# Expert weights of a routed mixture: loaded over one hardware DMA queue, or over two

## The chip, the cores and the metric

The kernel runs on one core of a Trainium2 chip. The metric is the device time of one execution, in microseconds. Before the change it is 2785.39 us, the median of three runs (2783.75 to 2786.51). A program on a single core has no other core to wait for.

## The reference, cut to what matters

The reference is a trunk of two layers. Each layer has a token mixer and then a mixture of 16 experts over 512 latent tokens and, in the first layer, also 256 context tokens. Everything is float32. The change is in the experts alone:

```
def ec_moe(h, w_router, w_gate, w_up, w_down):
    B, T, D = h.shape                            # D = 1024
    cap = EC_FACTOR * T // N_EXPERTS             # 64 latent tokens, 32 context tokens an expert
    aff = softmax(einsum('btd,de->bte', h, w_router))
    gate, idx = lax.top_k(swapaxes(aff, 1, 2), cap)
    xe = h[idx]
    hid = silu(einsum('becd,edf->becf', xe, w_gate)) * einsum('becd,edf->becf', xe, w_up)
    ye = einsum('becf,efd->becd', hid, w_down) * gate[..., None]
    return zeros(T, D).at[idx].add(ye)
```

Each expert has three matrices of 1024 x 1024 float32 (w_gate, w_up, w_down), 4 MB each, 12 MB in all. A layer reads 16 times 12 MB, and each expert's weights serve only 64 or 96 tokens.

## The kernel before, in words

The program is written engine by engine; an engine runs its own list in order and meets the others through semaphores alone. Nothing reorders the lists. The mixer, norms and routing take the stretches from 0 to about 970 us and from about 1510 to 2270 us of the span. The two expert phases lie at about 970 to 1510 us (layer 0, latent and context tokens) and 2270 to 2765 us (layer 1, latent tokens alone).

In an expert phase SBUF holds six slots of 2 MB. A slot s holds one half (512 rows) of one matrix of one expert, called a unit here and written (expert, slot): slots 0 and 1 hold the first and second half of w_gate, 2 and 3 those of w_up, 4 and 5 those of w_down. Slots 0 to 2 lie in the buffer `ring_lo`, slots 3 to 5 in `zone`, and rows of a profile name a unit by matrix and buffer. In layer 1 (`near_rows`) a unit is read as 16 KB pieces, in layer 0 as 4 KB pieces.

TensorE runs a hardware loop over the 16 experts (from `with pe.Fori(0, NE)`, helpers `in_half` and `out_half`, matmul lines L836 for gate and up, L846 for down). It takes the slots in the order 0 to 5. Before each it waits for `w_ready(s)`, which the transfer of the unit raises by 16; after each slot, or in layer 0 after each pair of slots, it raises `unit_done`. Between up and down stand the transposes of the hidden rows (L886) and those of the next expert's gathered tokens (L826). In layer 1 there are also eight small matmuls (`place`, L855) that put the previous expert's output rows in their places.

ScalarE's loop has few steps for each expert: the silu of the gate result (L1197, in layer 0 also L1201 for context tokens), the copy of the transposed hidden rows (L1203, raises `hidL`), and the scaled copy of the expert's output (L1208, in layer 0 also L1210, raises `ytm`). GpSimd issues the token gather (L1787) and, in layer 0, the scatter with addition (L1805); both are indirect DMAs on a queue of their own.

All weight transfers are issued by SyncE. Expert 0's six units are issued before the phase. Then comes the loop of L1923: for expert e and slot s it waits until `unit_done` says that expert e-1 has used slot s (L1925), then until the unit issued two before this one has landed (L1929; the semaphore of slot s-2), and issues the unit (L1912 in layer 0, L1910 in layer 1). So in this loop at most two units are under way at a time, both on SyncE's hardware queue (q1 in the profile). ScalarE has a hardware queue too (q10), which the mixer uses for 22 small transfers.

Of the kernel before, what the change touches and what calls it, by code (L numbers as in the profile page):

```python
# [14 lines left out]
P = 128  # L15
# [11 lines left out]
NE, FF = 16, 1024  # L27
# [47 lines left out]
def build(nc, A, out):  # L75
    ctx = ExitStack()
    with ctx:
# [5 lines left out]
        def sem(name):  # L83
            if name not in made:
                made[name] = ctx.enter_context(nc.semaphore(name))
            return made[name]
# [28 lines left out]
        def slot_ap(s):  # L115
            return ring_lo[:, s * SLOT:(s + 1) * SLOT] if s < 3 else zone[:, (s - 3) * SLOT:(s - 2) * SLOT]
# [70 lines left out]
        o = Z0  # L187
# [17 lines left out]
        o = Z0  # L205
# [14 lines left out]
        o = Z0  # L220
# [44 lines left out]
        def bank(j):  # L265
            return PS[j // 2][:, (j % 2) * 512:(j % 2) * 512 + 512]
# [21 lines left out]
        for l in range(DEPTH):  # L288
            n = [0]
# [14 lines left out]
            for q in range(12):  # L304
                c = C_BG + 256 * q
# [22 lines left out]
        def w_ready(s):  # L328
            return sem(f"w_ready{s}")
# [4 lines left out]
        def phase_end(eng, n):  # L334
            eng.drain().then_inc(sem("phase"), 1)  # L335
            eng.wait_ge(sem("phase"), 4 * n)
        NPH = 12

        def nt(l):
            return NT if l == 0 else LT  # L340
# [4 lines left out]
        def streams(l):  # L345
            return [(0, 0, S)] + ([(1, S, CTX)] if l == 0 else [])
# [9 lines left out]
        def near_rows(l):  # L356
            return l > 0
# [27 lines left out]
            return st  # L385

        POOL_ORDER = (3, 2, 1, 0)

        block = ctx.enter_context(nc.Block())

# [2 lines left out]
        def _(pe):  # L393
            mm, tr = nc.tensor.matmul, nc.tensor.transpose

            def unit(key):
                src, slot, count, _, _ = units[key]
                pe.wait_ge(w_ready(slot), 16 * count)
                return slot_ap(slot)
# [42 lines left out]
            for l in range(DEPTH):  # L442
# [31 lines left out]
                for n, (src, k) in enumerate([(src, k) for src in (hi_r, lo_r) for k in range(KD)]):  # L474
                    q = k % 4
                    for _, t0, tw in both():
                        i = mm(PS[3][32 * q:32 * q + 32, t0:t0 + tw], gw[:, k, :], src[:, k, t0:t0 + tw].bitcast(F32),
                               start=(n < 4), stop=(n >= 12), skip_group_check=True)
# [150 lines left out]
                def features(name, tag, g0, sts, free, order=range(KB)):  # L629
                    for half in range(2):  # L630
                        w = split_unit(l, name, half)
                        for f in order:
                            if half == 0 and free:
                                pe.wait_ge(sem(free), l * PER[free] + g0 + f - 3)
                            for _, t0, tw in sts:
                                for k in range(4):
                                    i = cols3(PS[f], 4 * half + k, k, f, t0, tw, w, half == 0 and k == 0, half == 1 and k == 3)
                            if half:
                                i.then_inc(sem(tag), 1)
                            elif f == order[-1]:  # L640
                                i.then_inc(sem("half"), 1)
                        released[l, name, half] = (tag, l * PER[tag] + g0 + KB) if half else \
                            ("half", l * PER["half"] + SPLITS.index((name, 0)) // 2 + 1)
# [86 lines left out]

                features("pu", "pup", 0, streams(l), None, POOL_ORDER)
                pe.wait_ge(sem("pw_in"), l * PER["pw_in"] + 16)
                for n, gi in enumerate(POOL_ORDER):
                    pe.wait_ge(sem("pin"), l * PER["pin"] + n + 1)
# [182 lines left out]
        def _(act):  # L917
# [17 lines left out]
            for l in range(DEPTH):  # L935
# [64 lines left out]
                for j in range(NT):  # L1000
                    c = FW[j]
# [19 lines left out]
                for n in range(12):  # L1021
                    r, c = n % 2, (FW, BWD)[n % 2][n // 2]
# [104 lines left out]

                for n, f in enumerate(POOL_ORDER):
                    act.wait_ge(sem("pup"), l * PER["pup"] + n + 1)
# [3 lines left out]
                    act.drain().then_inc(sem("pu"), 1)  # L1133
                for n, gi in enumerate(POOL_ORDER):
                    act.wait_ge(sem("pmap"), l * PER["pmap"] + n + 1)
# [52 lines left out]

                ns = nslot[l]
                act.drain().then_inc(sem("ytm"), 1)  # L1190
                with act.Fori(0, NE) as e:
                    if first:
                        act.wait_ge(sem("gate_L"), e + 1)
                    else:
                        act.wait_ge(sem("unit_done"), l * PER["unit_done"] + 6 * e + 2)
                    act.wait_ge(sem("hid"), l * PER["hid"] + e + 1)
                    A_(gsil[:, 0:512], bank(2), ACT.Silu).then_inc(sem("gsil"), 1)  # L1197
                    if first:
                        act.wait_ge(sem("unit_done"), 6 * e + 2)
                        act.wait_ge(sem("hid_c"), e + 1)  # L1200
                        A_(gsil[:, 512:768], bank(4)[:, 0:256], ACT.Silu).then_inc(sem("gsil_c"), 1)  # L1201
                    act.wait_ge(sem("hid_T"), l * PER["hid_T"] + e + 1)
                    A_(hidL.rearrange("p b g m -> p (b g m)"), bank(6), ACT.Copy).then_inc(sem("hidL"), 1)  # L1203
                    act.wait_ge(sem("iprev"), l * PER["iprev"] + e + 1)
                    if first:
                        act.wait_ge(sem("ig_free"), e + 1)
                    act.wait_ge(sem("unit_done"), l * PER["unit_done"] + 6 * e + 6)
                    i = A_(ytm[:, 0:512], bank(3), ACT.Copy, scale=gcur[:, 0:1])  # L1208
                    if first:
                        i = A_(ytm[:, 512:768], bank(5)[:, 0:256], ACT.Copy, scale=gcur[:, 1:2])  # L1210
                    i.then_inc(sem("ytm"), 1)
                phase_end(act, ph + 12)
                for t in range(nt(l) + 1):
                    if t < nt(l):
# [16 lines left out]
        def _(dve):  # L1231
# [34 lines left out]
            for l in range(DEPTH):  # L1266
# [229 lines left out]
                dve.drain()  # L1496
                for n, gi in enumerate(POOL_ORDER):
                    w = WINDOWS[gi]
# [316 lines left out]
        def _(sp):  # L1815
# [20 lines left out]
            for l in range(DEPTH):  # L1836
# [61 lines left out]
                for s, t0, t1 in [(0, 0, LT), (1, LT, NT)][:len(streams(l))]:  # L1898
                    src = (A["x"][0], A["ctx"][0])[s] if l == 0 else x_dram[l]
                    sp.dma_start(x_sb[:, t0:t1, :], src.rearrange("(t p) d -> p t d", p=P)).then_inc(sem("x_back"), 16)  # L1900


                exp_src = [(A["w_gate"], 0), (A["w_gate"], 512), (A["w_up"], 0), (A["w_up"], 512),
                           (A["w_down"], 0), (A["w_down"], 512)]

                def expert_unit(e, s):
                    w, c = exp_src[s]
                    src = w[l][bass.ds(e, 1), c:c + 512, :]
                    if near_rows(l):
                        sp.dma_start(slot_ap(s), src.rearrange("o (p k) n -> p (o k n)", p=P)).then_inc(w_ready(s), 16)  # L1910
                    else:
                        sp.dma_start(slot_ap(s).rearrange("p (k n) -> p k n", k=4),  # L1912
                                     src.rearrange("o (k p) n -> p (o k) n", p=P)).then_inc(w_ready(s), 16)
                for s in range(6):
                    if s < 3:
                        sp.wait_ge(sem(last[s][0]), last[s][1])
                    elif s == 3:
                        sp.wait_ge(sem("phase"), 4 * (NPH * l + 9))
                    expert_unit(0, s)
                if near_rows(l):  # L1920
                    sp.wait_ge(sem("phase"), 4 * (NPH * l + 11))
                    sp.dma_start(iota, A["iota"]).then_inc(sem("iota_in"), 16)
                with sp.Fori(1, NE) as e:  # L1923
                    for s in range(6):
                        sp.wait_ge(sem("unit_done"), l * PER["unit_done"] + 6 * e + (s - 5))  # L1925
                        sp.sem_inc(sem("sp_turn"), 1)

                        s2, back = (s - 2) % 6, 1 if s < 2 else 0
                        sp.wait_ge(w_ready(s2), 16 * e + 16 * (moe_base[l][s2] + 1 - back))  # L1929
                        sp.sem_inc(sem("sp_turn"), 1)  # L1930
                        expert_unit(e, s)

                for s in range(6):
                    last[s] = ("unit_done", l * PER["unit_done"] + 6 * NE - 5 + s)
# [41 lines left out]
```

## Time and profile before

| | |
|---|---|
| median of the runs | 2785.39 us |
| profiled execution, its own time | 2786.34 us |
| span of its trace | 2784.6 us |
| mean granted TensorE clock | 0.942 |
| TensorE busy | 2431.1 us, 87% of the span |
| ScalarE busy | 616.1 us, 22% |
| bytes on SyncE's queue q1 | 561.18 MB |
| bytes on ScalarE's queue q10 | 5.31 MB |
| read from HBM | 574.53 MB |

The span runs from the first to the last instruction of the profiled execution; 1.7 us of its own time lie outside. A transfer's "us to landing" runs from its issue to the moment when its semaphore has the full count. Engine names: PE is TensorE's matmuls, PEld its weight loads, DVE VectorE, ACT ScalarE, POOL GpSimd, SPq and ACTq the instruction queues of SyncE and ScalarE. Where a row of TensorE has a bracket, the number in it is the idle time just before the row, with what ended it. PEclk is the share of full clock that TensorE was granted.

### The profile page before, as it was taken

The page shows a single profiled execution, that of the slowest core. Times are in us where ns is not written, and L with a number is a line of the kernel's source. Part 1 is how long each engine was busy: PE and PEld are TensorE (multiplying, and loading weights), DVE is VectorE, ACT ScalarE, POOL GpSimd, SP SyncE. Part 2 cuts the span into 40 slices and gives each one's busy share as a digit, 9 for nine tenths or more (in the row PEclk, how much of TensorE's full clock was granted, in tenths as well). Part 3 has the DMA queues.
Part 4 walks back from the last instruction along what each step waited for, and adds up shares of the span by engine and source line. Part 5 has one row for each costly group of instructions (what it writes and reads, how often), then busy time and mean ns, then how long its engine had stood idle before and what let it go on. Part 6 is the DMA issues. An engine that isn't in the chain of part 4 may idle for free.

```text
span 2784.6 us, 38818 instructions
## 1 busy us (share of the span) xinstructions
PE 2431.1 (87%) x16038; PEld 1540.2 (55%) x16038; DVE 729.7 (26%) x1401; ACT 616.1 (22%) x1038; POOL 551.8 (20%) x304
## 2 busy tenths in 40 slices
PE   3987979899999399999997597997899859988886
PEld 2766867788874244444443475776688433333332
DVE  3245035301001511111111426135210142322224
ACT  3233234322111211111111423233321121101011
POOL 1232231324420011111111223231455000000000
PEclk7999999999999699999998798999999979999998
DMA  6261331122140599999999245332223369999996
GB/s 225 88 232 61 121 99 35 46 68 68 48 156 0 207 347 387 389 391 391 390 390 362 89 150 194 82 99 72 68 91 99 109 268 403 410 411 403 408 409 263
DMA packets 177524, 593.92 MB, mean 213 GB/s; under 512 B 13928, under 2 KB 55280, under 8 KB 165040
## 3 DMA queue, kind: packets, MB, share of 16 engines
q1 hardware_dynamic: 164080, 561.18, 53.9%
q0 software_dynamic: 10304, 25.99, 3.4%
q10 hardware_dynamic: 3040, 5.31, 0.6%
q8 instruction: 76, 1.25, 0.2%
q14 instruction: 24, 0.20, 0.0%
HBM read 574.53 MB, written 21.05 MB: 214 GB/s over the span
## 4 chain that ended last, share of the span: by engine, by line
PE 47%; DMA 36%; issue 6%; DVE 5%; ACT 3%; SPq 1%; POOLq 1%; POOL 1%; DVEq 0%; ACTq 0%
PE ps L418 15%; DMA ring_lo<-in_w_gate 12%; DMA zone<-in_w_up 11%; DMA zone<-in_w_down 10%; PE ps L413 9%; PE ps L760 6%; PE ps L778 5%; PE ps L836 2%; PE ps L427 2%; PE ps L693 1%; DMA ring_lo<-in_ada_w 1%; PE ps L710 1%; POOLq L335 1%; PE ps L598 1%; DVE zone L1413 1%
## 5 line engine op out<-in xcount | busy, mean ns | idle before, releaser
L418 PE MATMUL ps<-hi_r,ring_r 128*128 128x512 f32 (+1 forms) x1792 | 477.0, 355 | 18.2 <-POOLq L335 14.8
L836 PE MATMUL ps<-ring_lo,zone 128*32 128x256 f32 (+1 forms) x3072 | 440.4, 494 | 31.1 <-DMA ring_lo<-in_w_gate 26.9
L418 PEld LDWEIGHTS ps<-hi_r,ring_r 128*128 128x128 f32 x1792 | 318.6, 191 | 67.1 <-POOLq L335 16.1
L1682 POOL TENSOR_TENSOR ring_r<-ring_lo,ring_r 128x2048 fp32r<-128x2048 f32 x52 | 239.6, 4610 | 482.2 <-ACT ring_r L929 481.8
L836 PEld LDWEIGHTS ps<-ring_lo,zone 128*32 128x32 f32 (+1 forms) x3072 | 156.9, 124 | 307.9 <-issue 280.3
L418 PE MATMUL ps<-lo_r,ring_r 128*128 128x512 f32 (+1 forms) x896 | 316.7, 353 | 0.0
L846 PE MATMUL ps<-zone 128*64 128x512 f32 (+1 forms) x2048 | 290.9, 495 | 0.9
L413 PE MATMUL ps<-ring_r,hi_r 128*128 128x512 f32 x736 | 234.5, 400 | 21.8 <-DVEq L335 21.8
L1787 POOL DMA_INDIRECT zone<-xn_dram,zone x36 | 40.5, 1124 | 860.0 <-DVE zone L1654 773.4
L846 PEld LDWEIGHTS ps<-zone 128*64 128x64 f32 (+1 forms) x2048 | 110.9, 125 | 164.0 <-issue 143.7
L418 PEld LDWEIGHTS ps<-lo_r,ring_r 128*128 128x128 f32 x896 | 170.7, 190 | 23.5
L413 PEld LDWEIGHTS ps<-ring_r,hi_r 128*128 128x128 f32 x736 | 138.3, 192 | 51.1 <-DVEq L335 22.1
L1528 DVE TENSOR_TENSOR zone<-zone,ps 128x768 f32<-128x768 f32 (+1 forms) x48 | 39.4, 821 | 427.3 <-ACT zone L1159 427.3
L836 PE MATMUL ps<-zone 128*32 128x256 f32 (+1 forms) x1024 | 146.9, 487 | 2.7 <-DMA zone<-in_w_up 2.7
L413 PE MATMUL ps<-ring_r,lo_r 128*128 128x512 f32 x368 | 145.5, 395 | 0.0
L778 PE MATMUL ps<-ring_lo,zone 128*128 128x512 f32 x320 | 137.7, 592 | 0.0
L1614 DVE TENSOR_TENSOR zone<-zone,ps 128x512 f32<-128x512 f32 x136 | 84.3, 681 | 198.9 <-PE ps L855 198.8
L760 PE MATMUL ps<-br_lo,ring_r 128*128 128x512 f32 (+1 forms) x480 | 126.4, 355 | 0.0
L929 ACT ACTIVATE ring_r<-ring_lo 128x2048 fp32r<-128x2048 f32 x48 | 91.6, 1914 | 132.4 <-DMA ring_lo<-in_w_in 111.7
L760 PE MATMUL ps<-br_up,ring_r 128*128 128x512 f32 (+1 forms) x384 | 104.2, 358 | 3.8 <-DVE br_lo L1520 3.8
L778 PEld LDWEIGHTS ps<-ring_lo,zone 128*128 128x128 f32 x320 | 60.6, 190 | 75.8 <-issue 75.8
L836 PEld LDWEIGHTS ps<-zone 128*32 128x32 f32 (+1 forms) x1024 | 52.5, 123 | 90.2 <-issue 79.2
(272 smaller groups left out, 2584.7 us busy)
## 6 DMA issues: line engine op xcount, KB each, us to landing
ring_lo<-in_w_gate SPq DMA_DIRECT2D x64, 2048.0 KB, 10.9
zone<-in_w_down SPq DMA_DIRECT2D x64, 2048.0 KB, 10.1
ring_lo<-in_w_up SPq DMA_DIRECT2D x32, 2048.0 KB, 11.7
zone<-in_w_up SPq DMA_DIRECT2D x32, 2048.0 KB, 11.6
ring_lo<-in_w_in SPq DMA_DIRECT2D x52, 1024.0 KB, 5.3
ring_lo<-in_ada_w SPq DMA_DIRECT2D x24, 2048.0 KB, 11.7
ring_lo<-in_w_branch SPq DMA_DIRECT2D x24, 512.0 KB, 6.3
zone<-v_dram SPq DMA_DIRECT2D x128, 64.0 KB, 2.0
```

Of the source, the lines that this page charges most:

```text
L413: i = mm(dst, a[:, k, t * P:(t + 1) * P], b[:, kk, :], start=start and n == 0, stop=stop and n == 2)
L418: i = mm(dst[:, t0:t0 + tw], b[:, kk, f * P:(f + 1) * P], a[:, k, t0:t0 + tw], start=start and n == 0, stop=stop and n == 2)
L427: i = mm(bank(b)[32 * q:32 * q + 32, (j % 4) * P:(j % 4 + 1) * P], csil[:, k, :], w[:, k, q * P:(q + 1) * P], start=(k == 0), stop=(k == K ...
L760: i = mm(pb[:, t0:t0 + tw], w[:, k, (f % 2) * P:(f % 2 + 1) * P], b[:, k, t0:t0 + tw], start=(k == 0 and x == 0), stop=(k == KB - 1 and x ...
L778: i = mm(PS[2 + t % 2][:, j * 512:(j + 1) * 512], acc[:, k, t * P:(t + 1) * P], w[:, k, :], start=(k == 0), stop=(k == KD - 1))
L836: i = mm(bank(((2, 4), (3, 5))[s // 2][gi])[j * M:(j + 1) * M, 0:W], xeT[:, k, c0:c0 + M], w[:, k % 4, j * W:(j + 1) * W], start=(k == 0), ...
L846: i = mm(bank((3, 5)[gi])[j * M:(j + 1) * M, 0:W], hidL[:, k % 4, k // 4, :] if gi == 0 else hidC[:, k % 2, k // 2, :], w[:, k % 4, j * W: ...
L929: A_(unit_hi(slot, ring_r), unit_lo(slot), ACT.Copy).then_inc(sem("w_hi"), 1)
L1528: V.tensor_tensor(dst[:, 0:TW(l)], sg[f % 2][:, 0:TW(l)], PS[(f % 2) * 2][:, 0:TW(l)], ALU.mult).then_inc(sem("mg_free"), 1)
L1614: i = V.tensor_tensor(xn[:, t, 512 * j:512 * j + 512], xn[:, t, 512 * j:512 * j + 512], bank(HOT_BANKS[t % 2][j]), ALU.add)
L1682: G.tensor_tensor(unit_lo(slot, ring_r), unit_lo(slot), unit_hi(slot, ring_r).bitcast(F32), ALU.subtract)\
L1787: G.indirect_dma_start(xe[0:ns, :], None, xn_dram[l][0:TW(l), :], bass.IndirectOffsetOnAxis(ap=icur[0:ns, 0:1], axis=0)).then_inc(sem("xe_ ...
```

## The change: which engine issues which unit

The helper `expert_unit` moves out of SyncE's block, so that two engines can call it. SyncE's loop now issues only slots 0, 2 and 4; its two waits are written as before, so the unit of slot s-2 is now the one that SyncE itself issued last. ScalarE issues slots 1, 3 and 5 of the next expert at three points of its loop: slot 1 behind the silu, slot 3 behind the copy that raises `hidL` and a wait for `unit_done`, slot 5 behind the copy that raises `ytm`. These three have no wait for a landing. Expert 0 is still issued by SyncE, and ScalarE's last expert stands outside the loop, without transfers.

```
+        def expert_unit(eng, l, e, s):
+            w, c = exp_src[s]
+            src = w[l][bass.ds(e, 1), c:c + 512, :]
...
-                with act.Fori(0, NE) as e:
+
+                def expert(e, more):
...
+                    if more:
+                        expert_unit(act, l, e + 1, 1)
                     act.wait_ge(sem("hid_T"), l * PER["hid_T"] + e + 1)
                     A_(hidL.rearrange("p b g m -> p (b g m)"), bank(6), ACT.Copy).then_inc(sem("hidL"), 1)
+                    if more:
+                        act.wait_ge(sem("unit_done"), l * PER["unit_done"] + 6 * e + 4)
+                        expert_unit(act, l, e + 1, 3)
...
                     i.then_inc(sem("ytm"), 1)
+                    if more:
+                        expert_unit(act, l, e + 1, 5)
+                with act.Fori(0, NE - 1) as e:
+                    expert(e, True)
+                expert(NE - 1, False)
...
                 with sp.Fori(1, NE) as e:
-                    for s in range(6):
+                    for s in (0, 2, 4):
                         sp.wait_ge(sem("unit_done"), l * PER["unit_done"] + 6 * e + (s - 5))
                         sp.sem_inc(sem("sp_turn"), 1)
 
                         s2, back = (s - 2) % 6, 1 if s < 2 else 0
                         sp.wait_ge(w_ready(s2), 16 * e + 16 * (moe_base[l][s2] + 1 - back))
                         sp.sem_inc(sem("sp_turn"), 1)
-                        expert_unit(e, s)
+                        expert_unit(sp, l, e, s)
```

On SyncE the loop of layer 1 stood in this order before (`w_ready0` is the landing of slot 0, and so on):

```order
L1929 ISA [waits unit_done]
L1910 ISA [waits w_ready4]
L1910 DMA ring_lo<-in_w_gate 128x4096
L1925 REGISTER_ALU
L1910 ISA [waits unit_done,w_ready5]
L1910 DMA ring_lo<-in_w_gate 128x4096
L1925 REGISTER_ALU
L1929 REGISTER_ALU [waits unit_done]
L1910 DMA ring_lo<-in_w_up 128x4096 [waits w_ready0]
```

The same place of SyncE after the change:

```order
L1941 ISA [waits unit_done]
L396 ISA [waits w_ready4]
L396 DMA ring_lo<-in_w_gate 128x4096
L1937 REGISTER_ALU
L1941 REGISTER_ALU [waits unit_done]
L396 DMA ring_lo<-in_w_up 128x4096 [waits w_ready0]
L1937 REGISTER_ALU
L1941 REGISTER_ALU [waits unit_done]
L396 DMA zone<-in_w_down 128x4096 [waits w_ready2]
```

Between the transfers into slots 0 and 2 stood the one into slot 1; it is gone, while slot 2 still waits for slot 0's landing, slot 4 for slot 2's and slot 0 for slot 4's.

ScalarE's loop of layer 1 before:

```order
L1197 ACTIVATE zone<-ps 128x512 [waits hid]
L1202 REGISTER_ALU
L1203 ACTIVATE zone<-ps 128x512 [waits hid_T]
L1207 REGISTER_ALU [waits iprev]
L1208 ACTIVATE zone<-ps,zone 128x512 [waits unit_done]
```

ScalarE's loop of layer 1 after the change:

```order
L1210 ACTIVATE zone<-ps 128x512 [waits hid]
L396 ISA
L396 DMA ring_lo<-in_w_gate 128x4096
...
L1218 ACTIVATE zone<-ps 128x512 [waits hid_T]
L1220 REGISTER_ALU
L396 DMA zone<-in_w_up 128x4096 [waits unit_done]
L1225 REGISTER_ALU [waits iprev]
L1226 ACTIVATE zone<-ps,zone 128x512 [waits unit_done]
L396 DMA zone<-in_w_down 128x4096
```

A transfer now stands behind each of the three compute steps, and each waits in ScalarE's list for what stands ahead of it.

## Rows read from the trace of the kernel before

**Rows 1.** The page: 40 slices of 69.6 us, and the chain by engine.
```profile
GB/s 225 88 232 61 121 99 35 46 68 68 48 156 0 207 347 387 389 391 391 390 390 362 89 150 194 82 99 72 68 91 99 109 268 403 410 411 403 408 409 263
PE 47%; DMA 36%; issue 6%; DVE 5%; ACT 3%; SPq 1%; POOLq 1%; POOL 1%; DVEq 0%; ACTq 0%
```
**Rows 2.** Timeline, SyncE's issues in layer 1: start us, duration, queue, line, transfer, count.
```profile
2279.71 3.70 SPq L1910 DMA_DIRECT2D ring_lo<-in_w_gate  x2
...
2515.42 0.33 SPq L1910 DMA_DIRECT2D zone<-in_w_up  x1
2520.31 5.23 SPq L1910 DMA_DIRECT2D zone<-in_w_down  x2
...
2719.45 5.21 SPq L1910 DMA_DIRECT2D ring_lo<-in_w_gate  x2
```
**Rows 3.** Timeline, SyncE's issues in layer 0.
```profile
978.87 2.02 SPq L1912 DMA_DIRECT2D ring_lo<-in_w_gate  x2
...
1236.36 0.37 SPq L1912 DMA_DIRECT2D zone<-in_w_up  x1
1241.48 7.21 SPq L1912 DMA_DIRECT2D zone<-in_w_down  x2
...
1459.23 5.47 SPq L1912 DMA_DIRECT2D ring_lo<-in_w_gate  x2
```
**Rows 4.** Timeline, TensorE: hidden-row transposes once an expert, and waits for weights.
```profile
1224.63 0.66 PE L886 MATMUL ps<-cst,zone 128*128 128x128 f32 x4
1258.05 0.66 PE L886 MATMUL ps<-cst,zone 128*128 128x128 f32 x4
...
1454.02 3.65 PE L836 MATMUL ps<-zone 128*64 128x512 f32 x16 [0.56 <-DMA zone<-in_w_up]
...
2350.40 0.72 PE L886 MATMUL ps<-cst,zone 128*128 128x128 f32 x4 [1.06 <-DVE zone L1645]
2378.17 0.72 PE L886 MATMUL ps<-cst,zone 128*128 128x128 f32 x4 [1.06 <-DVE zone L1645]
...
2547.05 5.35 PE L836 MATMUL ps<-ring_lo,zone 128*64 128x512 f32 x16 [2.10 <-DMA ring_lo<-in_w_gate]
```
**Rows 5.** Line view of L1910 (layer 1): issue to landing.
```profile
DMA to landing us min/median/max: 7.8/9.7/31.3
```
**Rows 6.** Line view of L1912 (layer 0): issue to landing.
```profile
DMA to landing us min/median/max: 7.9/11.7/32.3
```
**Rows 7.** Windows: busy us (count) by engine, then PEclk, DMA share, GB/s.
```profile
2506.00:2511.00 5.00, 3.81 (x18) 1.15 (x16) 0.15 (x1) 0.69 (x1) 0.00 (x0) 1.00 1.01 308
2512.00:2529.00 17.00, 14.96 (x68) 4.85 (x66) 5.51 (x10) 1.88 (x2) 0.00 (x0) 1.00 1.01 428
1220.00:1230.00 10.00, 9.95 (x102) 5.03 (x100) 3.54 (x8) 0.60 (x1) 0.95 (x1) 1.00 1.03 410
1677.00:1680.00 3.00, 2.06 (x20) 1.80 (x22) 1.63 (x5) 1.73 (x7) 2.28 (x2) 1.00 1.04 398
1680.00:1682.00 2.00, 1.26 (x18) 0.93 (x16) 1.93 (x5) 1.53 (x6) 0.00 (x0) 1.00 1.06 396
```
**Rows 8.** Timeline, ScalarE's queue in the mixer of layer 1: one load issued.
```profile
1676.45 0.33 ACTq L979 DMA_DIRECT2D zone<-u_dram  x1
```
**Rows 9.** DMA issues by line: KB each, median us to landing.
```profile
zone<-u_dram ACTq DMA_DIRECT2D x20, 256.0 KB, 6.5
zone<-in_iota SPq DMA_DIRECT2D x1, 256.0 KB, 2.6
```
**Rows 10.** Timeline, ScalarE in one expert of layer 1.
```profile
2520.46 0.60 ACT L1197 ACTIVATE zone<-ps 128x512 f32<-128x512 f32 x1
2531.89 0.60 ACT L1203 ACTIVATE zone<-ps 128x512 f32<-128x512 f32 x1 [10.83 <-PE ps L886]
2540.02 0.69 ACT L1208 ACTIVATE zone<-ps,zone 128x512 f32<-128x512 f32 x1 [7.53 <-PE ps L846]
```
**Rows 11.** Line view of L1912: duration of the issuing instruction, ns min/median/max.
```profile
L1912 SPq DMA_DIRECT2D zone<-in_w_down x32: 372/373/4780, 906.9 to 1488.4; - x32
```

More of the change, by code:

```diff
@@ L387, in build @@
         POOL_ORDER = (3, 2, 1, 0)
+        exp_src = [(A["w_gate"], 0), (A["w_gate"], 512), (A["w_up"], 0), (A["w_up"], 512),
+                   (A["w_down"], 0), (A["w_down"], 512)]
+        def expert_unit(eng, l, e, s):
+            w, c = exp_src[s]
+            src = w[l][bass.ds(e, 1), c:c + 512, :]
+            if near_rows(l):
+                eng.dma_start(slot_ap(s), src.rearrange("o (p k) n -> p (o k n)", p=P)).then_inc(w_ready(s), 16)
+            else:
+                eng.dma_start(slot_ap(s).rearrange("p (k n) -> p k n", k=4),
+                              src.rearrange("o (k p) n -> p (o k) n", p=P)).then_inc(w_ready(s), 16)
         block = ctx.enter_context(nc.Block())
@@ L1900, in _ @@
                     sp.dma_start(x_sb[:, t0:t1, :], src.rearrange("(t p) d -> p t d", p=P)).then_inc(sem("x_back"), 16)
[L1903 to L1913, printed above, removed]
                 for s in range(6):
@@ L1918, in _ @@
                         sp.wait_ge(sem("phase"), 4 * (NPH * l + 9))
-                    expert_unit(0, s)
+                    expert_unit(sp, l, 0, s)
                 if near_rows(l):
```

## The prediction

> **What bounds the kernel now.** I read the page's slices first. GB/s shows two plateaus, 387 to 391 and 403 to 411, which are the two expert phases, and the chain puts 36% of the span on DMA [rows 1]. The change is in these phases alone, so the question is whether their pace is set by TensorE, by the transfers, or by the waits between them.
>
> The pace of the transfers comes from SyncE's issues. In layer 1 the first unit of an expert is issued at 2279.71 for expert 1 and at 2719.45 for expert 15 [rows 2]: 439.7 us over 14 experts, 31.4 us each. In layer 0 it is 978.87 and 1459.23 [rows 3]: 480.4 over 14, 34.3 us each. The pace of TensorE comes from its transposes, once an expert. Where it waits for no weights it takes 33.4 us an expert in layer 0 (1224.63 to 1258.05) and 27.8 in layer 1 (2350.40 to 2378.17) [rows 4]. So transfers set the pace in both phases, by 0.9 us an expert in layer 0 and by 3.6 in layer 1. TensorE lives on the units loaded ahead at first, then waits: 0.56 us for a half of w_up late in layer 0, 2.10 for the second half of w_gate in layer 1 [rows 4].
>
> Are the DMA engines full, then, or only late? Full: in layer 1 they stand at a share of 1.01 and 428 GB/s for 17 us on end, in layer 0 at 1.03 and 410 [rows 7]. Two units under way at a time suffice for that: the next issues follow 4.89 us apart (2515.42 to 2520.31) [rows 2], 5.12 in layer 0 [rows 3]. Six such units are 29.3 of the 31.4 us, and 30.7 of the 34.3. The other 2.1 and 3.6 us belong to the gathers and scatters: 308 GB/s in a stretch with a gather [rows 7].
>
> **What a second queue can bring.** No engine time is free for it: the share is 1.01 already. The mixer shows both hardware queues at work: a stretch of weights moves 398 GB/s, and the next, in which a small load of ScalarE's queue is under way beside them, 396 [rows 7, 8]. I take 0 for mixing the two, gain or loss; ends: 3% less, and for the better what the gathers lose, below. The Trainium skill says the same of bandwidth ("DMA: Bandwidth & Descriptors", section "Issuing engines are not separate DMA queues"): transfers of all issuing engines run on the same 16 DMA engines and interleave. By that rule this term is 0 as well, and the second queue adds no bandwidth.
>
> **What is moved on ScalarE.** Three issues an expert, at 0.33 to 0.37 us each by SyncE's rows [rows 2, 3], with a few register operations: about 1.3 us of ScalarE an expert. It is idle 10.83 us before the copy of the hidden rows and 7.53 before that of the output [rows 10], so this lies beside other work: 0. If an issue met a full queue, it could hold ScalarE for 4.78 us, the longest in layer 0 [rows 11]; that is a rival below. The points of issue are a few us later than the moment at which each slot is free (the silu ends 5.6 us after the matmuls of slot 1 began: 2515.4 to 2521.1), but still long before the use.
>
> **What is removed: the second unit under way on SyncE's queue.** This is the term that counts. The wait for the landing of slot s-2 meant "the one before the last"; now that SyncE issues every second slot, it means "the last". So SyncE has one unit under way, and from each landing on its queue is empty until the next is issued and its first bytes move. The price: the fastest unit took 7.8 us from issue to landing in layer 1 [rows 5] and 7.9 in layer 0 [rows 6], against 4.89 and 5.12 us of moving. A gap of 2.9 and 2.8 us, three an expert: 8.7 and 8.4 us in which SyncE's queue moves nothing. Before, the second unit covered each gap. Now only ScalarE's queue can.
>
> ScalarE's queue has three units an expert, 3 x 4.89 = 14.7 us of engine time in layer 1, and no throttle. Where both queues hold work I let each move half; the trace has no row for the split, only a small transfer that takes 6.5 us on ScalarE's queue beside weights on the other, where one of the same size takes 2.6 alone [rows 9], so it neither waits for the 10 us of units ahead on the other queue nor has the engines to itself. (The Trainium skill, same page, section "Queues, rings and completion order", has each DMA engine go round between the queues packet by packet. If the first queue were served first instead, ScalarE's units would move in the gaps alone, and the sum would be nearer 31.4 an expert.)
>
> Let f be the share of the gaps that ScalarE's queue covers. The period is T = 31.4 + 8.7(1-f). That queue moves 8.7f of its work in gaps, at full speed, and the rest at half speed, so it is busy 8.7f + 2(14.7 - 8.7f) = 29.4 - 8.7f. Its units are issued at moments that TensorE's progress sets, at about 2521.1, 2532.5 and 2540.7 [rows 10], and SyncE's gaps fall where its landings fall; taking the two as unrelated, f is busy over T. That gives f = 0.68 (23.5 busy in 34.2): **T = 34.1, 2.7 us more an expert**. In layer 0: T = 34.3 + 8.4(1-f), busy 30.7 - 8.4f, f = 0.68, T = 37.0, again 2.7 more. Ends: f = 1 costs 0; f = 0 costs 8.7 and 8.4.
>
> Both phases are at the pace of the transfers when they end, and each expert after the first is loaded in the loop, so all of it reaches the span: 15 x 2.7 + 15 x 2.7 = **81 us**.
>
> **The clock.** TensorE will wait 34.1 - 27.8 = 6.3 us an expert in layer 1 and 3.6 in layer 0. After a wait of 2.10 us the first matmuls took 5.35 us instead of 3.65 [rows 4]: 1.7 us at a lower granted clock. Behind a transfer pace this was hidden; now ScalarE's issues hang on TensorE's progress, so part of it is passed on. Ends 0 and 30 x 1.7 = 51; I take 8 of 30 experts, 14 us, nearer to 0, since rows of the longer kind are the fewer.
>
> **The sum**, on the profiled execution's own 2786.3: + 81 + 14 = 2881. That execution is 1 us over the median, so **2880 us**, 3.4% slower. A measurement of this kernel can tell about 0.2%, 5.6 us, from no change.
>
> **Rivals.**
> Covered gaps: ScalarE's three units are issued early (slot 1's as soon as the gate result is out) and without a throttle, so its backlog could span every gap, f at 0.95 or more. Then T grows by at most 0.4 us: 2785 to 2797. For it: its queue is busy 29 us of 31 if all is shared. Against: what it moves in gaps ends its backlog sooner. 13%, about half of it within 0.2%.
>
> Faster: the queue that is added fills what the gathers lose. A stretch with a gather moves 308 instead of 428 GB/s [rows 7]; 2.1 us an expert in layer 1, of which the gather's own 64 rows of 4 KB need 0.6 at 428 GB/s. With a third queue's packets in line 1.5 us could come back, 15 x 1.5 = 22 us, and 15 x 0.3 = 4 in layer 0, whose waits are that short: 2785 - 26 = 2759. It decides only if SyncE's gaps stay covered, too. 7%.
>
> Starved: gaps fall just where ScalarE's queue is empty, since both hang on TensorE: it waits for a first half, so ScalarE issues nothing, so the queue drains. With f near 0.2, 15 x (7.0 + 6.7) = 205, up to 2990; from f = 0.4 on it passes 2915. For it: an even half share makes the first half of a matrix, needed sooner, land after up to 9.8 us of moving instead of 4.9, while second halves of the next expert take the other half. 15%.
>
> Blocked: an issue on ScalarE meets a full queue, 4.8 us once an expert [rows 11], holding the silu: 30 x 4.8 = 144, 2929. Against: at most three of its own units are under way. 3%.
>
> **How the numbers follow.** Forecast 62%, with f between 0.5 and 0.9 and the clock's ends: 2812 to 2940. The range of 80% goes to 2805 below and 2945 above. Slower by over 0.2%: 0.62 + 0.15 + 0.03 + 0.06 of the covered case = 0.86; within 0.2%: 0.07; faster: 0.07.
>
> **What the profile after would show.** SyncE's issues into slot 0 come 34 and 37 us apart instead of 31.4 and 34.3; GB/s in the plateaus falls to about 376 and 362 (408 x 31.4/34.1, 391 x 34.3/37.0), with DMA share under 1 in short windows behind SyncE's landings. TensorE's waits for weights name first halves (slots 0, 2) and are 3 to 6 us an expert; none for second halves. ScalarE's issues take about 0.35 us each, and no compute step behind them is late. Median us to landing rises for SyncE's units from 9.7 to 10 or more though only one is under way. The mixer doesn't change. I am wrong if the DMA share stays at 1.0 through the phases: then the gaps were covered, or a second queue carries more than the 428 GB/s seen.

## The result, and the profile after

The changed kernel takes 2897.05 us (median of 4 runs, 2887.78 to 2909.64), the kernel before 2785.95 in the same comparison: a ratio of 1.0401, with a 95% interval of 1.0354 to 1.0448. The profiled execution took 2903.4 us, its span is 2901.5; it is 6 us over the median, so its trace shows a loss of 117 us where the medians have 111. The prediction was 2880, so the sign and the mechanism stood, and the loss was 111 us instead of the 95 forecast.

The page of the changed kernel, slices of 72.5 us, against [rows 1]:

```profile
DMA  6261431122224599999997263331324488999995
GB/s 216 84 237 44 130 95 41 44 66 66 73 102 188 188 386 357 341 345 356 357 354 262 90 228 107 87 93 43 109 88 138 181 336 348 360 362 367 348 377 196
PE 44%; DMA 38%; issue 6%; DVE 5%; ACT 3%; SPq 1%; POOLq 1%; POOL 1%; DVEq 0%; ACTq 0%
```

The plateaus of 387 to 391 and 403 to 411 GB/s have become 341 to 357 and 348 to 377 (forecast: 362 and 376). The pace of the transfers, from SyncE's issues into slot 0 for experts 1 and 15, against [rows 3] and [rows 2] (timeline of SyncE; first layer 0, then layer 1):

```profile
979.30 0.40 SPq L398 DMA_DIRECT2D ring_lo<-in_w_gate  x1
...
1508.55 0.37 SPq L398 DMA_DIRECT2D ring_lo<-in_w_gate  x1
...
2329.11 0.35 SPq L396 DMA_DIRECT2D ring_lo<-in_w_gate  x1
...
2832.88 0.33 SPq L396 DMA_DIRECT2D ring_lo<-in_w_gate  x1
```

Over 14 experts that is 37.8 us each in layer 0 (34.3 before) and 36.0 in layer 1 (31.4 before). The stretch of layer 0 grew by 48.9 us and that of layer 1 by 64.0. Together with 3.5 us at the end of layer 1 and 0.4 at the start they are the difference of the spans, 116.9, to 0.1 us. The mixer between the two phases lost nothing: from the last of these issues in layer 0 to the first in layer 1 it is 820.6 us, and 820.5 before.

One pass through layer 1 shows how. In the rows of the changed kernel L396 (layer 0: L398) issues a unit, L848 is the matmuls of gate and up, L858 those of down, L898 the transposes of the hidden rows; on ScalarE L1210 is the silu, L1218 the copy that raises `hidL`, L1226 the copy of the output. The timeline of SyncE and of ScalarE (its last number is the wait before a row):

```profile
2608.39 0.33 SPq L396 DMA_DIRECT2D zone<-in_w_down  x1
2620.72 0.33 SPq L396 DMA_DIRECT2D ring_lo<-in_w_gate  x1
2636.36 0.33 SPq L396 DMA_DIRECT2D ring_lo<-in_w_up  x1
```

```profile
2605.47 0.34 ACTq L396 DMA_DIRECT2D ring_lo<-in_w_gate  x1
2606.55 0.60 ACT L1210 ACTIVATE zone<-ps 128x512 f32<-128x512 f32 x1
2619.36 0.60 ACT L1218 ACTIVATE zone<-ps 128x512 f32<-128x512 f32 x1 [12.21 <-PE ps L898]
2619.50 0.34 ACTq L396 DMA_DIRECT2D zone<-in_w_up  x1
2627.75 0.69 ACT L1226 ACTIVATE zone<-ps,zone 128x512 f32<-128x512 f32 x1 [7.79 <-PE ps L858]
2627.81 0.34 ACTq L396 DMA_DIRECT2D zone<-in_w_down  x1
```

The windows view of three stretches in it (busy us and count by engine, then PEclk, DMA share, GB/s):

```profile
2608.00:2611.00 3.00, 2.62 (x13) 1.10 (x15) 0.73 (x2) 0.00 (x0) 0.00 (x0) 1.00 0.98 415
2612.00:2616.00 4.00, 4.00 (x20) 1.44 (x20) 2.78 (x6) 0.00 (x0) 0.00 (x0) 1.00 1.00 426
2618.00:2623.00 5.00, 4.20 (x24) 2.68 (x26) 1.80 (x4) 0.60 (x1) 1.35 (x1) 1.00 0.67 220
```

At 2608.39 SyncE's slot 2 has landed and slot 4 is issued. ScalarE's queue has two units, so this gap is covered (415 GB/s), and then both queues move (426). Slot 4 lands at about 2620.5. ScalarE's queue had run dry; its next unit was issued at 2619.50, since TensorE came to its transposes only then. Both queues start from nothing, and the DMA engines stand at 0.67 and 220 GB/s for 5 us. That is an uncovered gap.

The place is typical. Below are windows from 2 us before to 3 us behind three issues of SyncE that follow each other, into slots 0, 2 and 4:

```profile
2726.44:2731.44 5.00, 3.94 (x24) 2.32 (x24) 2.13 (x4) 0.60 (x1) 0.73 (x1) 1.00 0.47 125
2739.66:2744.66 5.00, 3.01 (x8) 1.12 (x10) 0.00 (x0) 0.00 (x0) 0.00 (x0) 0.50 0.98 373
2751.39:2756.39 5.00, 4.62 (x22) 1.65 (x20) 2.48 (x4) 1.68 (x2) 0.00 (x0) 1.00 0.92 318
```

Over all 15 experts of the loop in layer 1 the DMA share of such a window is under 0.9 at 12 issues into slot 0, 1 into slot 2 and 4 into slot 4; in layer 0 at 9, 0 and 4. The engines run empty mostly behind the landing of slot 4.

The waits of TensorE for weights in layer 1 (waits view, 2310 to 2880: us in total, times, longest), against the longest of 2.10 us in [rows 4]:

```profile
PE ps L848 <- DMA ring_lo<-in_w_gate: 40.1, 9, 9.1
PE ps L848 <- DMA ring_lo<-in_w_up: 30.8, 11, 5.2
...
PE ps L858 <- DMA zone<-in_w_down: 0.2, 1, 0.2
```

The half of w_up named is the one in `ring_lo`, the first. No wait names the second half of w_up, which lies in `zone`. Both halves of w_gate lie in `ring_lo`; there the timeline tells them apart, since each of the nine waits stands before a row that holds the 32 matmuls of both halves, as here:

```profile
2457.91 9.66 PE L848 MATMUL ps<-ring_lo,zone 128*64 128x512 f32 x32 [9.11 <-DMA ring_lo<-in_w_gate]
```

So TensorE waits for first halves alone, 4.7 us an expert in layer 1. In layer 0 it is the same by its timeline, with 2.6 us an expert (38.3 us in 14 waits for w_gate and w_up, against 2.7 in all before).

### The profile page after: what moved, and what is told of

Its sections match the earlier page's. It is cut to its first block, busy times and chain, and to the rows that moved or that the text cites. A ratio compares the mean times of both kernels' runs of the same rounds, so it can differ in the third digit from the quotient of the medians.

```text
span 2901.5 us, 38524 instructions
## 1 busy us (share of the span) xinstructions
PE 2469.9 (85%) x16038; PEld 1557.5 (54%) x16038; DVE 729.7 (25%) x1401; ACT 613.0 (21%) x1036; POOL 551.6 (19%) x304
## 4 chain that ended last, share of the span: by engine, by line
PE 44%; DMA 38%; issue 6%; DVE 5%; ACT 3%; SPq 1%; POOLq 1%; POOL 1%; DVEq 0%; ACTq 0%
PE ps L430 15%; DMA ring_lo<-in_w_up 14%; DMA ring_lo<-in_w_gate 12%; DMA zone<-in_w_down 11%; PE ps L425 8%; PE ps L772 5%; PE ps L790 5%; PE ps L848 2%; PE ps L439 2%; PE ps L705 1%; DMA ring_lo<-in_ada_w 1%; PE ps L722 1%; POOLq L335 1%; PE ps L610 1%; DVE zone L1436 1%
## 5 line engine op out<-in xcount | busy, mean ns | idle before, releaser
L848 PE MATMUL ps<-ring_lo,zone 128*32 128x256 f32 (+1 forms) x3072 | 473.2, 518 | 113.6 <-DMA ring_lo<-in_w_up 56.6
L848 PEld LDWEIGHTS ps<-ring_lo,zone 128*32 128x32 f32 (+1 forms) x3072 | 172.7, 130 | 409.1 <-issue 381.7
L858 PE MATMUL ps<-zone 128*64 128x512 f32 (+1 forms) x2048 | 296.0, 501 | 2.2 <-DMA zone<-in_w_down 1.4
L858 PEld LDWEIGHTS ps<-zone 128*64 128x64 f32 (+1 forms) x2048 | 112.5, 126 | 168.9 <-issue 148.7
L848 PE MATMUL ps<-zone 128*32 128x256 f32 (+1 forms) x1024 | 146.9, 487 | 0.0
L1218 ACT ACTIVATE zone<-ps 128x512 f32<-128x512 f32 x32 | 19.1, 597 | 429.6 <-PE ps L898 429.6
```

The costliest lines, as they stand in the source:

```text
L848: i = mm(bank(((2, 4), (3, 5))[s // 2][gi])[j * M:(j + 1) * M, 0:W], xeT[:, k, c0:c0 + M], w[:, k % 4, j * W:(j + 1) * W], start=(k == 0), ...
L858: i = mm(bank((3, 5)[gi])[j * M:(j + 1) * M, 0:W], hidL[:, k % 4, k // 4, :] if gi == 0 else hidC[:, k % 2, k // 2, :], w[:, k % 4, j * W: ...
```

## The experiments

**Two units under way on SyncE's queue.** The changed kernel, with the wait for a landing moved one unit back:

```
-                        s2, back = (s - 2) % 6, 1 if s < 2 else 0
+                        s2, back = (s - 4) % 6, 1 if s < 4 else 0
```

> SyncE's wait now names the landing of its unit before the last, so two of its units may be under way; ScalarE's three issues stay as they are. Gap theory: the gaps of SyncE's queue are covered by its own second unit, f is 1, and the loss goes: 2786 (2780 to 2795), slot 0's issues 31.4 and 34.3 us apart again, DMA share 1.0 through both phases, though each queue still has only half of the engines. Rival, sharing: the loss comes from first halves that land late because the next expert's second halves take half of the engines; then deeper queues change little and it stays near 2880 to 2910. Rival, mixing: two hardware queues move fewer bytes than one; then it stays over 2820 with the DMA share at 1.0 and GB/s under 400 in layer 1.

Measured: 2791.23 us, ratio 1.0016 (1.0002 to 1.0029) to the kernel before. Its windows, layer 0 and layer 1:

```profile
1010.00:1470.00 460.00, 454.73 (x4124) 198.41 (x4122) 53.13 (x139) 52.44 (x81) 54.46 (x41) 1.00 1.03 389
2360.00:2740.00 380.00, 339.19 (x1518) 121.81 (x1514) 93.59 (x181) 38.66 (x49) 16.18 (x12) 0.98 1.01 408
```

Nearly the whole loss is gone by one index, with two queues, ScalarE's issues and the sharing all in place. So neither the sharing nor a poorer throughput of two queues is the cause: the engines are at 1.03 and 1.01, with 389 and 408 GB/s, as in the same windows of the kernel before.

**No wait for a landing at all.** The changed kernel, without these lines of SyncE's loop:

```
-                        s2, back = (s - 2) % 6, 1 if s < 2 else 0
-                        sp.wait_ge(w_ready(s2), 16 * e + 16 * (moe_base[l][s2] + 1 - back))
-                        sp.sem_inc(sem("sp_turn"), 1)
```

> SyncE waits for free slots alone, for no landing. Gap theory: as with two under way, 2786 (2775 to 2795); what is left over is whether more outstanding units fill what the gathers lose: if so up to 26 us less, 2760. Sharing: 2880 to 2910 as the changed kernel. Blocked issues: with more units in SyncE's queue an issue may stand for some us, which costs nothing on SyncE.

Measured: 2789.91 us, ratio 1.0020 (1.0008 to 1.0032). The same as with two under way. The hope of 26 us from filling the gathers' losses is refuted for two queues.

**The gap by itself.** The kernel before, one queue, each unit waiting for the one right before it:

```
-                        s2, back = (s - 2) % 6, 1 if s < 2 else 0
+                        s2, back = (s - 1) % 6, 1 if s < 1 else 0
```

> The kernel before, all units on SyncE's queue, but each issue waits for the landing of the unit right before it: one under way, no other queue. It measures the gap by itself. Gap theory: six uncovered gaps an expert, 6 x 2.9 = 17.4 us in layer 1 and 6 x 2.8 = 16.8 in layer 0, so slot 0's issues are 48.8 and 51 us apart and the time is 2786 + 15 x 34.2 = 3299 (3200 to 3400). Sharing: a lone queue has nobody to share with, so the time is near 2786, over it by the issue latencies at most (under 2850).

Measured: 3300.16 us (2 runs), ratio 1.1849 (1.1820 to 1.1877), against the 3299 expected. Three issues of layer 1 that follow each other (timeline of SyncE), and the line view of L1910:

```profile
2741.15 0.33 SPq L1910 DMA_DIRECT2D ring_lo<-in_w_up  x1
2748.98 0.33 SPq L1910 DMA_DIRECT2D zone<-in_w_up  x1
2756.87 0.33 SPq L1910 DMA_DIRECT2D zone<-in_w_down  x1
```

```profile
DMA to landing us min/median/max: 7.6/7.9/31.0
```

They are 7.8 and 7.9 us apart, where two under way made it 4.89 [rows 2]: a gap of 2.9 to 3.0 us each, with no second queue in play. The price of a lone gap, taken from one minimum of the trace, was right.

**The halves swapped.** The changed kernel, ScalarE with slots 0, 2, 4, SyncE with 1, 3, 5:

```
-                        expert_unit(act, l, e + 1, 1)
+                        expert_unit(act, l, e + 1, 0)
...
-                    for s in (0, 2, 4):
+                    for s in (1, 3, 5):
```

> The changed kernel with the roles swapped: ScalarE issues slots 0, 2 and 4 at its three points, SyncE slots 1, 3 and 5 with one under way. Gap theory: the gaps are as many and as long, so 2860 to 2920, with TensorE now waiting for second halves. Sharing and urgency: the halves needed first are now those issued early and without a throttle, so most of the loss goes: 2790 to 2830.

Measured: 2886.49 us, ratio 1.0360 (1.0335 to 1.0385). Its waits in layer 1:

```profile
PE ps L848 <- DMA ring_lo<-in_w_gate: 77.5, 14, 6.6
PE ps L898 <- DVE zone L1668: 13.8, 13, 1.1
PE ps L848 <- DMA zone<-in_w_up: 37.1, 13, 5.8
```

The wait for w_up has moved from its first half (`ring_lo`) to its second (`zone`), while the loss stayed at 90% of the changed kernel's. Which half travels on which queue decides for what TensorE waits, hardly for how long.

**More and less cover.** Two kernels that change how many gaps there are and how much work ScalarE's queue has for them. First, ScalarE issues slots 1, 3, 4 and 5, SyncE 0 and 2:

```
                     if more:
+                        expert_unit(act, l, e + 1, 4)
                         expert_unit(act, l, e + 1, 5)
...
-                    for s in (0, 2, 4):
+                    for s in (0, 2):
...
-                        s2, back = (s - 2) % 6, 1 if s < 2 else 0
+                        s2, back = (2, 1) if s == 0 else (0, 0)
```

> The changed kernel, but ScalarE issues slot 4 too (right before slot 5), so SyncE has two units an expert (slots 0 and 2), still one under way. Gap theory: two gaps an expert, 5.8 us, and four units (19.6 us of engine time) on ScalarE's queue to cover them; the formula's busy time is 39.1 - 5.8f, over the period, so f is 1: 2786 to 2800. If f is smaller than the formula has it, as in the changed kernel (0.5 to 0.6 there instead of 0.68), it is about 0.8 and costs 15 x 2.3 = 35 us: 2820. Sharing: ScalarE's queue takes half of the engines for longer, so slots 0 and 2 land later: over 2900.

Measured: 2790.29 us, ratio 1.0021 (1.0008 to 1.0033). Second, ScalarE issues slots 1 and 5, SyncE 0, 2, 3 and 4, each behind the landing of the one before:

```
-                    if more:
-                        act.wait_ge(sem("unit_done"), l * PER["unit_done"] + 6 * e + 4)
-                        expert_unit(act, l, e + 1, 3)
...
-                    for s in (0, 2, 4):
+                    for s in (0, 2, 3, 4):
...
-                        s2, back = (s - 2) % 6, 1 if s < 2 else 0
+                        s2, back = {0: (4, 1), 2: (0, 0), 3: (2, 0), 4: (3, 0)}[s]
```

> The changed kernel, but SyncE issues slots 0, 2, 3 and 4 (one under way, each waits for the landing of the one before) and ScalarE only slots 1 and 5. Gap theory: four gaps an expert, 11.6 and 11.2 us, with 9.8 and 10.2 us of work to cover them; the formula gives f = 0.39, periods of 38.5 and 41.1, 2786 + 15 x (7.1 + 6.8) = 2995; with f as far below the formula as in the changed kernel, 3050. Sharing: SyncE's units have the engines to themselves for longer, so it is faster than the changed kernel: 2820 to 2880.

Measured: 3011.37 us, ratio 1.0817 (1.0789 to 1.0845). The formula of the prediction had 2786 to 2800 and 2995; with f as far below the formula as in the changed kernel it would have been 2820 and 3050, and neither came. Sharing had the opposite order: over 2900 for the first, 2820 to 2880 for the second. It is refuted both ways. The first of the two still has only one unit of SyncE under way, and loses almost nothing: what matters is not the wait as such but whether other work stands in the DMA queues through it.

The three kernels with two queues and the loss gone (two under way, no wait, four units on ScalarE's queue) are still 0.16 to 0.21% slower than the kernel before, and none of the three intervals reaches 1. What takes these 5 us or so is not shown.

**The change in layer 1 alone.**

```
-                    for s in (0, 2, 4):
+                    for s in (range(6) if l == 0 else (0, 2, 4)):
```

(ScalarE's loop of layer 0 issues nothing.)

> The change in layer 1 alone; in layer 0 SyncE issues all six slots, two under way, as before. In the changed kernel's trace layer 1 lost 64 us (slot 0 of expert 1 to slot 0 of expert 15: 503.8 us instead of 439.7) and all before it 49. If the two phases lose independently of each other: 2786 + 64 = 2850 (2840 to 2862). If the loss of one phase is the other's (a delayed start, a colder clock at its beginning), it is well off that: under 2830 or near 2897.

Measured: 2848.31 us, ratio 1.0229 (1.0206 to 1.0252): 64 us (57 to 70 by the interval), as read from the changed kernel's trace. In the trace of this run slot 0's stretch in layer 0 is 480.0 us, as in the kernel before, and that in layer 1 497.2, which is 57.5 us more; so the agreement to 1 us is partly chance. Within that spread the two phases lose independently.

**More under way on one queue.** The kernel before with three units under way, and with no wait for a landing:

```
-                        s2, back = (s - 2) % 6, 1 if s < 2 else 0
+                        s2, back = (s - 3) % 6, 1 if s < 3 else 0
```

> The kernel before, with three units under way on SyncE's queue instead of two. Gap theory: two already cover every gap, so nothing changes: 2780 to 2790. If what the gathers lose could be filled by more units under way on the same queue, up to 26 us less: 2760.

> The kernel before without the wait for a landing: all units on SyncE's queue, as many under way as slots are free. Three under way gave a ratio of 0.9984 to the kernel before. If the small gain comes from more units under way beside the gathers, it stays or grows: 2775 to 2782. If three was enough, the same as three: 2781. If it was chance, 2785. A cost would show as SyncE's issues held for some us in a full queue, which nobody waits for.

Measured: 2781.09 us, ratio 0.9984 (0.9974 to 0.9994), and 2781.61 us, ratio 0.9986 (0.9975 to 0.9997). Layer 1 with three under way, where the kernel before has 408 GB/s in the same window:

```profile
2310.00:2740.00 430.00, 391.03 (x1760) 139.80 (x1758) 110.50 (x213) 46.18 (x58) 18.82 (x14) 0.98 1.01 413
```

By their ratios both are 4 us faster than the kernel before, and so than both kernels. That is twice the same small gain in separate comparisons, so I take it as real, though each interval ends within 0.1% of no change. With no wait layer 1 moves 410 GB/s in the same window. Whether the gain lies in the stretches with gathers was not followed up. The 26 us that the gathers might have given back did not come on one queue either.

## Why the prediction was right, and where its size was off

**Bounds.** Right. Transfers set the pace in both phases, and all they lost reached the span.

**Bandwidth of a second queue.** Right at 0 for a full queue: 426 GB/s with both queues at work, against 428 with one [rows 7].

**Each queue moves half.** Right. The DMA view of 2612 to 2616 in the changed kernel (queue, packets, MB, share of the 16 engines):

```profile
q1 hardware_dynamic: 55, 0.90, 52.9%
q10 hardware_dynamic: 49, 0.80, 47.1%
```

**ScalarE's issues.** Right: 0.34 us each in layer 1, and the two copies behind them still wait for TensorE, 12.21 and 7.79 us in the pass above against 10.83 and 7.53 before [rows 10]. The longest of ScalarE's 90 issues took 0.45 us, so none was held by a full queue; the rival of blocked issues is out.

**The gap.** Right for a lone queue, 2.9 us. Beside a busy one it was undersized; of the terms of the sum, this is the one measured off its size. SyncE issued at 2608.39, while ScalarE's queue was moving. The DMA view of the 3 us that follow has no packet of q1:

```profile
q10 hardware_dynamic: 95, 1.29, 101.5%
```

In the kernel with four units on ScalarE's queue, an issue at 2505.20 met the same, here to 2508.70:

```profile
q10 hardware_dynamic: 110, 1.54, 103.5%
q1 hardware_dynamic: 1, 0.02, 1.1%
```

With no other traffic the first packets came between 0.9 and 1.5 us after the issue; this is the kernel before, issue at 2279.71 [rows 2], view of 2279.71 to 2281.21:

```profile
q1 hardware_dynamic: 14, 0.23, 77.6%
```

So a gap next to a busy queue can be over 2 us longer. It is not so every time. Read packet by packet, the 45 issues of SyncE's loop in layer 1 of the changed kernel have their first packet after 0.95 to 1.0 us in 18 cases, 1.4 to 2.2 in 4, and 2.7 to 4.2 in 23, with a mean of 2.4; the 90 of the kernel with one queue one deep all have it after 0.96 to 1.04. An issue at 2457.91, while ScalarE's queue was near the end of its last unit, had packets of both queues within 1.5 us:

```profile
q10 hardware_dynamic: 39, 0.49, 77.3%
q1 hardware_dynamic: 6, 0.10, 22.3%
```

The mean gap was therefore about 2.9 + 1.4 = 4.3 us in layer 1, and by the same reading (means of 2.5 and 1.1 us) about 4.3 in layer 0: an estimate of 12.9 us an expert instead of 8.7 and 8.4. While the late queue waits, the other moves, so the added time is covered, but it draws on the backlog of ScalarE's queue, which is then empty sooner. In the prediction's formula 4.3 us gives 36.6 us in layer 1 (measured 36.0) and 39.7 in layer 0 (measured 37.8). The direction fits; the size is too large, and more so elsewhere: already 4.0 us gives 3104 for the kernel in which SyncE issues four units, which took 3011. The formula takes gaps and issues as unrelated, and they are not, as the windows around slot 0 show.

**f, the covered share.** Forecast 0.68 in both layers. By the measured periods and the lone gap it was 1 - 3.5/8.4 = 0.58 in layer 0 and 1 - 4.6/8.7 = 0.47 in layer 1. By the measured gap of 4.3 us it was 0.73 and 0.64, close to the forecast. So the share was about right and the length it applies to was not, as far as the loss is the gaps' own. For the gaps the forecast had 2.7 us an expert, 76 us for the 14 experts of both stretches; the trace has 48.9 + 64.0 = 113, which contains whatever the clock added.

**The clock.** The granted clock did fall, windows of the kernel before and of the changed one in layer 1 (the two numbers ahead of the last are PEclk and DMA share):

```profile
2310.00:2740.00 430.00, 388.25 (x1742) 138.92 (x1740) 109.02 (x210) 44.38 (x57) 18.83 (x14) 0.98 1.01 408
```

```profile
2360.00:2850.00 490.00, 404.97 (x1720) 145.52 (x1722) 109.08 (x210) 44.30 (x56) 18.89 (x14) 0.91 0.92 361
```

In layer 0 it fell from 1.00 to 0.97 between slot 0 of expert 1 and slot 0 of expert 15. TensorE was busy 17 us longer in that stretch (477.6 to 494.8) and 19 us longer in the one of layer 1 (399.7 to 418.8). That makes 36 us an estimate of the most that a lower clock can have passed on, where the sum had 14. If all of it was passed on, 77 of the 113 us are left for the gaps, which is the forecast's 76; if none, 113. With one queue one deep the waits are longest, and the period of 49.8 us in layer 1 is only 1 us over the lone-gap sum; but there every issue waits for a landing, and none hangs on ScalarE. No run here separates the clock from the longer gap, so how the missing 16 us of the forecast divide between the two is open.

**The signs.** Slot 0's issues, the GB/s, ScalarE's issues, the mixer and waits for first halves alone came as forecast; the waits of 3 to 6 us an expert did so in layer 1 (4.7) but not in layer 0 (2.6). For the time to landing the page has these medians:

```profile
ring_lo<-in_w_gate SPq DMA_DIRECT2D x34, 2048.0 KB, 8.0
zone<-in_w_down SPq DMA_DIRECT2D x34, 2048.0 KB, 11.9
```

The 8.0 must not be read as slot 0's. The trace has landing times for only two of SyncE's transfers of w_gate, both of expert 0, ahead of a phase (8.0 and 8.1 us, issued at 905.80 and 2274.30); in the loop slot 0 and slot 2 have none. Slot 4 has them: a median of 10.2 us in layer 1, as forecast (10 or more), and 12.0 in layer 0, with one unit of SyncE under way.

**The rivals.** Covered gaps, faster, and blocked issues did not come true. Starved had a picture that came partly true: the engines run empty where ScalarE's queue has run dry because TensorE came late to its transposes. Its size did not: 205 us for f near 0.2, against 111.

**Slips in the working.** The upper end of the forecast, 2940, leaves out the clock's end: f of 0.5 costs 128 us and the clock's end 51, which is 2964. And f of 0.4 is 2939; 2915 is passed from f of 0.49 on. Neither touches the forecast of 2880.

## What to carry to other kernels

A wait that limits transfers under way is written here in units of one issuer's list. When the list is split, the same index means half the depth, and a queue that is one deep and has no other work beside it loses 2.9 us at every transfer here, against 4.9 us of moving. Count the units under way per queue before and after, and ask at each landing what else stands in the queues at that moment. Here the DMA engines showed a share of 1.0 already, and a second hardware queue added nothing; three units under way on one queue gave the little there was.

## What the runs showed of the hardware that was not expected

A transfer issued on an empty hardware queue starts late when the other hardware queue has a backlog. With four units an expert on ScalarE's queue, 28 of SyncE's 30 issues in layer 1 had their first packet 3.4 to 3.6 us later, while the other queue moved; alone, in the kernel with one queue one deep, all 90 had it after 0.96 to 1.04 us. In the changed kernel it lies anywhere from 0.95 to 4.2 us. What sets the delay was not tested. The pieces were 16 KB in all three. And the engines lose little in the mixing itself, 426 against 428 GB/s, once both queues are moving.
